# Conditioning vectors summed over partitions by TensorE transposes and a VectorE reduction, in place of products with a column of ones

## The reference

```python
    c_act = jax.nn.silu(c)
    for i in range(DEPTH_2):
        mod = c_act @ ada_w[i] + ada_b[i]          # 1024 -> 6144 numbers
        sh1, sc1, g1, sh2, sc2, g2 = jnp.split(mod, 6, axis=-1)
        h = modulate(rmsnorm_2(x, norm_gain[i, 0]), sh1, sc1)
        ...
        x = x + g1[:, None, :] * y
        h = modulate(rmsnorm_2(x, norm_gain[i, 1]), sh2, sc2)
        x = x + g2[:, None, :] * swiglu(h, ffn_w_gu[i], ffn_w_down[i])
```

## Time and profile before

| what | value |
|---|---|
| median of 3 runs | 2258.4 us |
| the profiled execution's own time | 2258.98 us |
| span of its instructions | 2257.2 us |
| PE busy | 2161.0 us, 96% |
| DVE busy | 1565.2 us, 69% |
| ACT busy | 1029.4 us, 46% |
| mean DMA rate | 211 GB/s |
| granted TensorE clock, mean | 0.989 |

### The profile page before, as it was taken

How to read it: one execution, slowest core, us unless ns; L and a number is a source line. 1 busy time by engine, 2 the same in 40 slices (tenths; PEclk the granted TensorE clock), 3 DMA queues, 4 the chain that set the end, 5 groups by cost and what they waited for, 6 DMA issues and landing times.

```text
span 2257.2 us, 33992 instructions
## 1 busy us (share of the span) xinstructions
PE 2161.0 (96%) x13827; PEld 1925.4 (85%) x13827; DVE 1565.2 (69%) x2153; ACT 1029.4 (46%) x1698; POOL 186.2 (8%) x202
## 2 busy tenths in 40 slices
PE   6899999999999999989999999999999999999997
PEld 5799888888998888767999787899898899778996
DVE  5477757766777577566898677899745896657444
ACT  5344445544444455455444444433445434464333
POOL 1000001101000011011001001001000001111000
PEclk9999999999999999999999999999999999999999
DMA  8876745566766445623899534699643697525651
GB/s 281 285 227 229 254 156 165 172 224 225 240 232 233 157 160 173 229 98 126 283 342 346 180 119 143 223 350 356 220 145 131 236 353 242 177 85 177 201 188 66
DMA packets 297104, 475.60 MB, mean 211 GB/s; under 512 B 19936, under 2 KB 151466, under 8 KB 296948
## 3 DMA queue, kind: packets, MB, share of 16 engines
q1 hardware_dynamic: 286548, 440.67, 57.5%
q0 software_dynamic: 10400, 32.76, 4.8%
HBM read 465.88 MB, written 7.47 MB: 210 GB/s over the span
## 4 chain that ended last, share of the span: by engine, by line
PE 87%; DVE 6%; DMA 2%; ACT 2%; issue 2%; POOL 1%; SPq 0%; DVEq 0%; POOLq 0%; ACTq 0%
PE G L138 68%; PE A L138 16%; PE G L141 2%; DVE pool L158 1%; DMA raw<-in_w_in 1%; DVE wlo L150 1%; DVE pool L150 1%; ACT pool L144 1%; POOL sm L150 1%; PE A L141 1%; DVE X L150 1%; ACT HTh L144 0%; DVE sm L155 0%; DMA pool<-mod_rows 0%; DMA pool<-in_ada_b 0%
## 5 line engine op out<-in xcount | busy, mean ns | idle before, releaser
L150 DVE TENSOR_TENSOR wlo<-raw,whi 128x1024 fp32r<-128x1024 f32 x640 | 774.2, 1238 | 199.7 <-ACT whi L144 198.2
L144 ACT ACTIVATE whi<-raw 128x1024 fp32r<-128x1024 f32 x640 | 646.3, 1054 | 211.4 <-DMA raw<-in_ffn_w_gu 91.8
L138 PE MATMUL G<-HTh,whi 128*128 128x256 f32 x2336 | 671.9, 288 | 12.0 <-DVE wlo L150 7.0
L138 PE MATMUL G<-HTh,wlo 128*128 128x256 f32 x2336 | 661.6, 283 | 0.0
L138 PE MATMUL G<-HTl,whi 128*128 128x256 f32 x2336 | 661.5, 283 | 0.0
L138 PEld LDWEIGHTS G<-HTh,whi 128*128 128x128 f32 x2336 | 448.4, 192 | 19.6 <-DVE wlo L150 10.8
L138 PEld LDWEIGHTS G<-HTl,whi 128*128 128x128 f32 x2336 | 448.7, 192 | 2.1
L138 PEld LDWEIGHTS G<-HTh,wlo 128*128 128x128 f32 x2336 | 448.3, 192 | 0.0
L144 ACT ACTIVATE pool<-G 128x512 f32<-128x512 f32 (+2 forms) x208 | 115.4, 573 | 537.6 <-PE G L138 504.3
L138 PE MATMUL G<-whi,HTh 128*128 128x512 f32 (+1 forms) x784 | 314.7, 401 | 26.3 <-DVE wlo L150 14.4
L138 PE MATMUL G<-whi,HTl 128*128 128x512 f32 (+1 forms) x784 | 304.6, 389 | 4.5 <-DVE HTl L158 4.1
(11 more groups left out here) (196 smaller groups left out, 2241.1 us busy)
## 6 DMA issues: line engine op xcount, KB each, us to landing
raw<-in_ada_w SPq DMA_DIRECT2D x192, 512.0 KB, 5.9
raw<-in_ffn_w_gu SPq DMA_DIRECT2D x352, 256.0 KB, 4.9
raw<-in_w_in SPq DMA_DIRECT2D x128, 512.0 KB, 4.5
raw<-in_ffn_w_down SPq DMA_DIRECT2D x88, 512.0 KB, 6.6
raw<-in_w_in SPq DMA_DIRECT2D x160, 256.0 KB, 4.8
raw<-in_swa_w_in SPq DMA_DIRECT2D x24, 512.0 KB, 5.3
pool<-mod_rows POOLq DMA_DIRECT2D x24, 512.0 KB, 6.4
raw<-in_gla_w_in SPq DMA_DIRECT2D x24, 512.0 KB, 5.2
```

The costliest lines, as they stand in the source:

```text
L138: return self.e.matmul(out, a, b, start=start, stop=stop, skip_group_check=True) if self.e else self
L144: return self.e.activation(out, a, func, bias=bias, scale=scale, accum_out=accum) if self.e else self
L150: return self.e.tensor_tensor(out, a, b, op) if self.e else self
```

## The change

TensorE no longer multiplies by ones. It transposes the four quarters of `acc` into one bank (128 x 512), and DVE adds each quarter up along its row with one `tensor_reduce` into four scratch columns, and then adds the bias from there. The DVE part is put in the list `soon` with a count of 1. The bank is marked as held between the two, `ada_sums` now asks for two free banks rather than one, and the planner's clock of the bank is set to DVE's clock when the reduction is written.

```diff
     def ada_sums(self, age=6):
-        while self.adaq and self.steps - self.adaq[0][4] >= age and not all(self.gheld):
+        while self.adaq and self.steps - self.adaq[0][4] >= age and self.gheld.count(False) > 1:
             l, u, b, acc, _ = self.adaq.pop(0)
             g = self.gbank()
             summed, m = ("pe_ada", (l, u)), ("ve_mod", (l, u))
-            self.h_ada_sum(g, b, acc, self.gfree[g], summed, l, u, m)
+            self.h_ada_tr(g, b, acc, self.gfree[g], summed)
             b.release([summed])
-            self.gfree[g] = [m]
-            if u == 11:
-                self.h_amod(l, m, ("ve_mod", (l, "a")))
-                self.modq.append(l)
+            self.gheld[g] = True
+
+            def total(l=l, u=u, g=g, summed=summed, m=m):
+                self.h_ada_sum(g, summed, l, u, self.smc(4), m)
+                self.gfree[g], self.gheld[g], self.gage[g], self.bclk[g] = [m], False, max(self.gage) + 1, self.clk["DVE"]
+                if u == 11:
+                    self.h_amod(l, m, ("ve_mod", (l, "a")))
+                    self.modq.append(l)
+            self.soon.append([1, total])
...
-    def h_ada_sum(self, g, b, acc, free, summed, l, u, done):
+    def h_ada_tr(self, g, b, acc, free, summed):
...
-        e.wait_ge(*self.at(self.tconst))
+        e.wait_ge(*self.at(self.tid))
         for n in range(4):
-            mm = e.matmul(M.GB[g][:, n:n + 1], b.a[:, n * P:n * P + P], M.ones[:, :], True, True)
+            mm = e.transpose(M.GB[g][:, n * P:n * P + P], b.a[:, n * P:n * P + P], M.ident[:, :])
         mm.then_inc(*self.up(summed))
...
-    def h_ada_sum(self, g, b, acc, free, summed, l, u, done):
+    def h_ada_sum(self, g, summed, l, u, tot, done):
         e, M = self.e, self.M
         e.wait_ge(*self.at(summed))
         e.wait_ge(*self.at(self.tadb))
         m, c = l * 64 + u * 4, l * 48 + u * 4
-        e.tensor_tensor(M.mod[:, m:m + 4], M.GB[g][:, 0:4], M.adb[:, c:c + 4], ALU.add).then_inc(*self.up(done))
+        part = ("ve_mod", (l, u, "s"))
+        e.tensor_reduce(tot, M.GB[g][:, :].rearrange("p (n k) -> p n k", n=4), ALU.add).then_inc(*self.up(part))
+        e.wait_ge(*self.at(part))
+        e.tensor_tensor(M.mod[:, m:m + 4], tot, M.adb[:, c:c + 4], ALU.add).then_inc(*self.up(done))
```

More of the change, by code:

```diff
@@ L456, in h_none @@
         pass
-    h_load = h_memset = h_piece = h_split = h_rest = h_ada = h_ada_sum = h_mm = h_mm1 = h_none
+    h_load = h_memset = h_piece = h_split = h_rest = h_ada = h_ada_tr = h_ada_sum = h_mm = h_mm1 = h_none
     h_copy = h_silu = h_tanh = h_gate = h_square = h_rstd = h_mean = h_pow = h_rows = h_none
```

## The result

The changed kernel takes 2261.99 us (median of 13 runs, 2260.06 to 2264.6) against 2258.4 us (13 runs beside them, 2255.64 to 2259.86): a ratio of 1.0018, 95% interval 1.0009 to 1.0026. It is slower by 3.6 us where the prediction said faster by 3.6. The profiled execution took 2263.80 us, its span 2262.0.

The account below looks back on a forecast made before the run. PE was taken to bound the kernel (87% of the chain of waits). Attention +2.7 and feed-forward blocks -5.6, -3.4 and +2.7 summed to -3.6 us: 2254.8 us by the median, range 2248 to 2263.5, forecast's chance 0.6.

Parts of the forecast that it names:

- the ledger of the feed-forward blocks: 32 feed-forward sums: DVE's lag behind PE, less waits given back, held against `wlo` margins; -5.6, -3.4 and +2.7 us by block.
- 4.5 left, against ... 6.0 us. It holds: First feed-forward block: lag 11.1 less 6.6 given back, within the 6.0 us `wlo` margin, so no PE waiting, -5.6 us.
- given back: Feed-forward blocks: DVE's earlier waits for PE and ACT absorb its lag; 6.6, 2.9 and 0.5 us by block.
- DVE's waits can't be given back: Feed-forward blocks: late `raw` reloads keep DVE waiting for ACT; lag 11.1 us in the first two, total 2263.3 us; chance 0.2.
- the ledger's own deadline: Second feed-forward block: `wlo` piece used at 1580.48, lag 8.2 against 6.0 us margin; PE waits 2.2 us.
- The attention term: Sixteen dilated attention sums: +1.5, +1.2 and 0 us, together +2.7, between -7.5 and +5.8.
- the third sum: First attention stretch: PE's other bank is free at 173.5, against 173.55 before, so 0 us; the second stretch repeats it.
- The third block: Feed-forward, 8 sums: lag 7.6 less 0.5 against 0.6 us margin; PE waits 6.5 us, so +2.7 us.
- its rival: Third feed-forward block: PE's wait lets the clock fall to 1.2 GHz; 7 us at half speed cost +3.5 us; chance 0.05.
- The numbers of a single sum: Each of 48 sums: transposes save PE 0.47 us, the reduction gives DVE 0.71 us more.
- The faster rival: Feed-forward blocks: DVE's lag doesn't reach PE, so 32 sums keep 0.47 us each; -12.3 us, 2246.1 us; chance 0.15.
- the slower rival: Feed-forward blocks: DVE's waits can't be given back, over 6.0 us lag in the first block; +4.9 us in all; chance 0.2.

Follow-up runs that it names:

- e6: Changed kernel, but a feed-forward unit on TensorE waits for its second PSUM bank only before the first product that writes it: 2254.24 us, ratio 0.9975.
- e2: Changed kernel with products with ones again and the bias read from PSUM, keeping the changed kernel's places, held banks and bank clock: 2259.2 us, ratio 1.0001.
- e7: Changed kernel with four ScalarE copies with accumulating output a sum instead of the reduction, and VectorE adding the bias once a layer: 2253.05 us, ratio 0.9968.
- e1: Changed kernel without the reduction; DVE adds the bias to the first four columns of the transposes: 2242.31 us, ratio 0.9926.
- e10: Changed kernel with four ScalarE copies a sum instead of the reduction, and the count in `soon` 2 instead of 1: 2234.96 us, ratio 0.9891.
- e5: Changed kernel with products with ones again, and the VectorE operation that reads them held back by a count of 2 instead of 1: 2249.26 us, ratio 0.9954.
- e4: Changed kernel with the reduction done twice in a row on DVE: 2295.74 us, ratio 1.0154.
- e3: Changed kernel with the count 2 instead of 1 in `soon`, so reduction and bias stand one piece later on DVE: 2246.23 us, ratio 0.9941.

## Why the prediction was wrong

**The step that failed is the ledger of the feed-forward blocks**, in block 1 where it says "4.5 left, against ... 6.0 us. It holds". The block gave 1.4 us instead of 5.6, and block 2 gave 1.3 instead of 3.4. These two terms, 4.2 and 2.1 us, are 6.3 of the 7.2 between forecast and result. The deadline of the ledger can be followed to its piece. After the change its rows, the answer to the first pair of rows 13, are:

```profile
1229.17 2.05 DVE L150 TENSOR_TENSOR wlo<-raw,whi 128x1024 fp32r<-128x1024 f32 x1 [0.20 <-ACT whi L144]
...
1231.27 0.19 PEld L138 LDWEIGHTS G<-HTh,whi 128*128 128x128 f32 x1 [0.29 <-DVE wlo L150]
```

The 6.0 us of margin are down to 0.05 and PE waits 0.29 us there, after 0.41 us at 1207.27. So DVE's lag reached 6.0 + 0.7 = 6.7 us, not 4.5. Two things were wrong in it.

*A wait that can't be given back was given back.* Rows 10 have 2.4 us of waiting for `whi`, 1.65 of it in one piece. First the kernel before, then the same place in the changed kernel:

```profile
1185.64 1.48 DVE L150 TENSOR_TENSOR wlo<-raw,whi 128x1024 fp32r<-128x1024 f32 x1 [1.65 <-ACT whi L144]
```
```profile
1188.77 1.47 DVE L158 SCALAR_TENSOR_TENSOR pool<-pool,G 128x512 f32<-128x512 f32 x2
1190.27 0.63 ACT L144 ACTIVATE OTh<-pool 128x512 fp32r<-128x512 f32 x1 [4.12 <-DVE pool L158]
1190.81 2.94 ACT L144 ACTIVATE whi<-raw 128x1024 fp32r<-128x1024 f32 x3
...
1191.89 1.47 DVE L150 TENSOR_TENSOR wlo<-raw,whi 128x1024 fp32r<-128x1024 f32 x1 [1.65 <-ACT whi L144]
```

ScalarE works its queue in order: the gate's output `OTh` stands ahead of the splits, and it waits for VectorE's own gate. VectorE waits for a ScalarE that it has itself held up, 1.65 us before (1185.64) and 1.65 us after, although it is later. The waits for the gate's input, `pool<-pool,G`, behind TensorE, were given back as counted. This is read from the rows; no run tests it by itself. It takes 1.65 of the missing 2.2 us; the other 0.5 is a little more lag a sum (0.73 and 0.46 instead of 0.71 and 0.47) and what I can't place. It is half of the rival "DVE's waits can't be given back": its sign and its effect are right, its mechanism (a late reload of `raw`) isn't what these rows show.

*The margin was taken at the wrong deadline.* The ledger watched `wlo` alone. A unit's first product needs its banks too, and the gate's first operation on VectorE frees the last one. Before (the first row is the low part that the unit needs, ready at 1235.94):

```profile
1234.72 1.22 DVE L150 TENSOR_TENSOR wlo<-raw,whi 128x1024 fp32r<-128x1024 f32 x1 [1.28 <-ACT whi L144]
...
1237.37 1.48 DVE L158 SCALAR_TENSOR_TENSOR pool<-pool,G 128x512 f32<-128x512 f32 x2
```

The first of the two ends at about 1238.1 and the unit, piece 350, starts at 1242.46 (its weight load is among the rows of block 1 above): 4.4 us of margin at a place where `wlo` had 6.5. After, with 6.7 us of lag, PE waits until the first of the two is done:

```profile
1244.26 1.48 DVE L158 SCALAR_TENSOR_TENSOR pool<-pool,G 128x512 f32<-128x512 f32 x2
...
1245.09 0.36 PE L138 MATMUL G<-HTh,whi 128*128 128x256 f32 x1 [1.90 <-DVE pool L158]
```

Block 1 then adds up: waits of 0.41 + 0.29 + 2.29 = 3.0 us and 1.4 us for the clock are 4.4, against 4.2 missing. The two errors work together. With the ledger's own 4.5 us, and 0.71 + 0.47 for one more sum on each engine before this point, the bank would have been late by 1.3 us at most (an estimate, 5.7 against 4.4), and `wlo` in time. e6 takes 2.3 of the 4.2 us back, the clock's fall among them; what it leaves is 0.6 us of waiting for `wlo` and 1.25 for the same bank.

In block 2 the ledger's own deadline came out near: PE waits 0.11 + 2.36 + 0.26 = 2.7 us up to 1581.46, where 2.2 were forecast. But the ledger stopped at that piece. PE waits another 1.75 us at 1594.72, and that is most of the 2.1 missing. At 1557 and at 1594 us it is the bank again that comes last (PE's six waits for the gate's operation, 9.4 us, all lie in the three blocks). e6 gives back only 0.3 here: PE waits 1.1 us for `wlo` and 2.6 for the bank.

**Right, with a size off.** The attention term: +2.7 forecast, +3.5 measured over the three rows that hold these sums (+2.1, +0.3 and +1.1), which scatter by some tenths. The five waits behind a sum of the first stretch came at +0.37 to +0.43. What was too low is the third sum: 0 forecast, +0.46 measured (1.61 - 0.69 - 0.46), in both stretches. "Free at 173.5" left out that the operation that frees the bank stands behind the sum on DVE and moves with it. The third block: +2.7 forecast, +3.1 measured, with 6.0 us of waiting where 6.5 were forecast. The clock fell there as its rival said, but e6 has no fall in this block and is no faster, so no part of the loss is shown to be the clock's.

**Right.** The numbers of a single sum: 0.46 us a sum on PE, 0.73 on DVE, DVE's busy time, no cost or gain from the new places (e2), waits for the sum in attention shorter by 0.35 us. The faster rival was wrong for this kernel. Its number is what e7 has in blocks 1 and 2, once VectorE is let off.

The observation named beforehand as speaking for the slower rival, a wait of PE in the first block, is what appeared. The Trainium skill's advice that speaks against the reduction ("VectorE: DVE Perf Modes", section "Rules for kernel authors") is borne out by its price here: some 20 us (e1) for 33.0 us of reductions. What stays open: why the row from 714 us, in which no sum stands, scatters by 2.7 us between kernels, and where the last 0.5 us of the lag in block 1 are from.

## What to carry to other kernels

Before idle time of an engine is counted as slack, follow its releaser one step further: a wait for a second engine that was itself waiting for the first came back in full here (1.65 us), though the first one was late. Where an engine's lag is held against a margin, list every thing that the bounding engine needs at that point, PSUM banks as well as operands, and take the earliest. Where a shorter operation on the bounding engine leaves a second half to do, the engine that gets it and its place decide what it is worth: the same transposes were 3.6 us slower than the kernel before with VectorE behind them, 6.8 us faster with ScalarE (e7), and 24.9 us faster with ScalarE one piece later (e10). Of that, 10.6 us are the later place alone, which the old products with ones have too (e5).

## What the runs showed of the hardware

- The granted clock fell to 0.50 for 3.4 us at the end of PE's waits of 2.29 and 3.03 us in the changed kernel, and in e4's first attention stretch at four of five waits of 2.2 to 2.7 us. It did not fall after one of 2.36 us (1557.46, the changed kernel), of 2.42 (1833.20, e6), or of 3.02 and 3.08 (1826.74 and 1847.50, e3); these are all waits of weight loads. One and the same wait, 2.66 us until 1268.39 in the kernel before and 2.67 us until 1271.91 in the changed one, left the clock at 1.00 in the first and was followed by a fall at 1272.7 in the second. So the length of a wait does not settle it; what does was not found out.
- What a fall of 3.4 us costs differs: 1.4 us in block 1, 5.9 us for four of them in e4's first attention stretch, and nothing that can be seen in block 3, where e6 without a fall is as slow.
- Transposes among products did not lower the clock: 1.00 in blocks 1 and 2 of e7 with 12 groups each.
- A ScalarE copy of 128x128 with an accumulating output takes two instructions, 264 and 186 ns; the accumulator's read is 40% of it. Four of them, 1.8 us, against 0.69 us for the one reduction on VectorE, and still the faster kernel.
